# One softmax loop over sixteen heads in a two-block transformer kernel, with its transpositions spread over the steps around it

## The reference

```python
def attn_mixer(h, w_in, ...):
    c_q, c_kv, k_r, q_b, k_b, v_b = jnp.split(h @ w_in, IN_SPLITS, axis=-1)
    q = rms_norm_2(c_q, g_cq) @ w_uq                 # 8 heads x 96, rope on 32
    kv = rms_norm_2(c_kv, g_ckv) @ w_ukv             # 8 heads x (64 + 64)
    ...
    q = rms_norm_2(q, g_qn_mla) * (MLA_QK ** -0.5)
    k = rms_norm_2(k, g_kn_mla)
    o_mla = causal_attention_blocks(q, k, v)
    qm = rms_norm_2(heads(q_b), g_qn_moba) * (MOBA_HEAD_DIM ** -0.5)
    km = rms_norm_2(heads(k_b), g_kn_moba)
    o_moba = moba_attention(qm, km, heads(v_b))      # with 256 tokens one block:
    return concat(o_mla, o_moba) @ w_o               # plain causal softmax attention
```

## Time and profile before

| what | value |
|---|---|
| median of 3 runs | 920.19 us (920.02 to 922.31) |
| the profiled execution's own time | 920.32 us |
| its span | 918.5 us, 12101 instructions |
| PE busy | 872.7 us (95%) |
| DVE, ACT, POOL busy | 573.6, 441.0, 106.9 us |
| mean granted clock of PE | 0.993 of full speed |

### The profile page before, as it was taken

One profiled execution on the slowest core, in us unless ns is written; L12 is line 12 of the kernel. 1 busy time (PEld: TensorE's weight loads), 2 busy tenths in 40 slices (PEclk: granted clock), 3 DMA queues, 4 the chain that ended last, 5 costly groups with the idle time before them and its releaser, 6 DMA issues.

```text
span 918.5 us, 12101 instructions
## 1 busy us (share of the span) xinstructions
PE 872.7 (95%) x5003; PEld 720.8 (78%) x5003; DVE 573.6 (62%) x707; ACT 441.0 (48%) x584; POOL 106.9 (12%) x73
## 2 busy tenths in 40 slices
PE   6999999898999999899999999999689999999997
PEld 5888788787887877778778777887678878888886
DVE  4685475775343768855777777776776565555552
ACT  5634466566853645534544445442154554444441
POOL 1000000211000013105033333331000000000000
PEclk9999999999999999999999999999799999999999
DMA  8826466353022627306446555656775555555521
GB/s 298 294 97 229 161 210 223 139 187 135 1 58 101 249 92 254 113 1 205 157 147 213 199 173 189 207 202 170 203 273 187 183 180 187 184 183 183 183 92 46
DMA packets 67248, 155.87 MB, mean 170 GB/s; under 512 B 3017, under 2 KB 6826, under 8 KB 66938
## 3 DMA queue, kind: packets, MB, share of 16 engines
q1 hardware_dynamic: 63888, 146.28, 46.7%
q0 software_dynamic: 2224, 7.67, 2.5%
q10 hardware_dynamic: 1082, 1.16, 0.6%
HBM read 146.70 MB, written 7.34 MB: 168 GB/s over the span
## 4 chain that ended last, share of the span: by engine, by line
PE 74%; DVE 15%; ACT 5%; issue 3%; DMA 2%; POOL 1%; ACTq 0%; DVEq 0%
PE bank L643 20%; PE bank L645 20%; PE bank L644 20%; DVE wlo L1454 4%; ACT whi L1112 2%; PE bank L636 2%; PE bank L744 1%; DMA ring<-in_w_in 1%; PE bank L904 1%; DVE wlo L1449 1%; DVE hT_lo L1437 1%; PE bank L955 1%; PE bank L787 1%; PE bank L717 1%; DVE work L1629 1%
## 5 line engine op out<-in xcount | busy, mean ns | idle before, releaser
L1454 DVE TENSOR_TENSOR wlo<-ring,whi 128x2048 fp32r<-128x2048 f32 (+1 forms) x105 | 255.2, 2434 | 162.3 <-ACT whi L1112 162.1
L1112 ACT ACTIVATE whi<-ring 128x2048 fp32r<-128x2048 f32 (+1 forms) x105 | 200.4, 1908 | 228.8 <-PE bank L645 187.0
L643 PE MATMUL bank<-whi,hT_hi 128*128 128x512 f32 (+1 forms) x736 | 291.2, 396 | 4.8 <-DVE hT_lo L2018 2.3
L645 PE MATMUL bank<-whi,hT_lo 128*128 128x512 f32 (+1 forms) x736 | 287.0, 390 | 0.0
L644 PE MATMUL bank<-wlo,hT_hi 128*128 128x512 f32 (+1 forms) x736 | 286.9, 390 | 0.0
L643 PEld LDWEIGHTS bank<-whi,hT_hi 128*128 128x128 f32 x736 | 139.0, 189 | 34.1 <-issue 3.5
L645 PEld LDWEIGHTS bank<-whi,hT_lo 128*128 128x128 f32 x736 | 138.7, 188 | 28.8
L644 PEld LDWEIGHTS bank<-wlo,hT_hi 128*128 128x128 f32 x736 | 139.1, 189 | 27.2 <-issue 0.2
L643 PE MATMUL bank<-whi,hidT_hi 128*128 128x512 f32 x256 | 100.6, 393 | 1.1 <-DVE hidT_lo L1955 1.1
L645 PE MATMUL bank<-whi,hidT_lo 128*128 128x512 f32 x256 | 99.7, 390 | 0.0
L644 PE MATMUL bank<-wlo,hidT_hi 128*128 128x512 f32 x256 | 99.7, 389 | 0.0
(11 more groups left out here) (273 smaller groups left out, 952.8 us busy)
## 6 DMA issues: line engine op xcount, KB each, us to landing
ring<-in_w_ff SPq DMA_DIRECT2D x64, 1024.0 KB, 5.3
ring<-in_ple_gate_w SPq DMA_DIRECT2D x8, 1024.0 KB, 5.2
ring<-in_w_kv SPq DMA_DIRECT2D x8, 1024.0 KB, 7.0
ring<-in_b_w_in SPq DMA_DIRECT2D x8, 1024.0 KB, 5.0
ring<-in_a_w_in SPq DMA_DIRECT2D x7, 1024.0 KB, 13.0
ring<-in_w_in SPq DMA_DIRECT2D x6, 1024.0 KB, 5.5
ring<-in_w_glu SPq DMA_DIRECT2D x6, 1024.0 KB, 6.3
ring<-in_a_w_out SPq DMA_DIRECT2D x4, 1024.0 KB, 5.8
```

Of the source, the lines that this page charges most:

```text
L643: pe.matmul(bank_cols, high[:, at[0], at[1]], w_high, start=first, stop=False)
L645: return pe.matmul(bank_cols, low[:, at[0], at[1]], w_high, start=False, stop=last)
L1112: act.activation(whi[at], raw_rows(g), ACT.Copy).then_inc(high_made, 1)
L1454: dve.tensor_tensor(wlo[at], raw_rows(g), whi[at], ALU.subtract).then_inc(low_made, 1)
```

## The change

- `AHEAD` is 3: the probabilities of head n are turned in step n + 3 (before, n + 2), and the values follow in step n + 4.
- One loop of 20 steps covers 16 heads, the MLA heads first. The MoBA heads' scores are made two at a time in the even steps 8 to 14, their products alternating between the upper and lower 64 rows.
- The MLA queries and keys are turned in pairs of heads: tiles 0 and 1 inside the product "wv", between the two token tiles of its second half (`amid`), tiles 2 and 3 at steps 1 and 2. ACT empties all query tiles, DVE all key tiles. The MoBA tiles are turned at steps 4 to 7, one a step, all in bank 7 and all emptied by ACT.
- ACT loads the table of the exponential ahead of `refill("wv", 0)` (`preload_act_table_set`).
- On DVE the squares of the MLA keys go ahead of `refill("wq", 1)`, the scaling of the MLA queries ahead of `refill("wk", 0)`, that of the MLA keys ahead of `refill("wk", 1)`; the means of the MoBA keys go ahead of the loop, and `refill("wv", 0)` moves from ahead of the loops to the end of step 10.
- The banks of "wv" are 2 and 3 (before, 1 and 2). The turn of the bank list has advanced less, so the output's turned tiles come to banks 1 to 4.

```diff
+AHEAD = 3
+MOBA_TURNS = {4: ("qmoba", 0), 5: ("qmoba", 1), 6: ("kmoba", 0), 7: ("kmoba", 1)}
...
+def soft_plan(u):
+
+    u.add(("wv", 0, 0), "a", bank=2)
+    for k in range(2):
+        u.add(("T", "qmla", k), "a", bank=4 + 2 * k)
+        u.add(("T", "kmla", k), "v", bank=5 + 2 * k)
+    u.add(("wv", 0, 1), "a", bank=3)
+    for i in range(2 * MH + AHEAD + 1):
+        if i < MH:
+            u.add(("scores", i), "a", bank=i % 4)
+        elif i < 2 * MH and i % 2 == 0:
+            u.add(("scores", i), "a", bank=i % 4)
+            u.add(("scores", i + 1), "a", bank=i % 4 + 1)
+        if i in (1, 2):
+            u.add(("T", "qmla", 1 + i), "a", bank=2 + 2 * i)
+            u.add(("T", "kmla", 1 + i), "v", bank=3 + 2 * i)
+        if AHEAD <= i < 2 * MH + AHEAD:
+            u.add(("probsT", i - AHEAD), "v", bank=4 + (i - AHEAD) % 2)
+        if i > AHEAD and (i - AHEAD - 1) % 4 == 3:
+            m = (i - AHEAD - 1) // 4
+            u.add(("soft_out", m), "v", bank=6 + m % 2)
+        if i in MOBA_TURNS:
+            name, k = MOBA_TURNS[i]
+            u.add(("T", name, k), "a", bank=7)
...
+                            if amid and t == 0:
+                                amid()
...
+            def early_turns():
+                soft_turns(0)
+                soft_turns(1)
+
+            product("wv", 0, "wv", amid=early_turns)
...
+            def moba_scores(i):
+
+                pair = [begin(("scores", i + odd)) for odd in range(2)]
+                rows = [slice(HD * odd, HD * odd + HD) for odd in range(2)]
+                c = (i - MH) // 2
+                tq, tk = turned_qk["moba"]
+                emptied(("T", "qmoba", c // 2))
+                emptied(("T", "kmoba", c // 2))
+                for b, r in zip(pair, rows):
+                    pe.matmul(b[:, 0:P], tq[r, c, 0:P], tk[r, c, 0:P], start=True, stop=False, skip_group_check=True)
+                for b, r in zip(pair, rows):
+                    pe.matmul(b[:, P:P + S], tq[r, c, P:S], tk[r, c, :], start=False, stop=False, skip_group_check=True)
+                for odd, b in enumerate(pair):
+                    score_masks(i + odd, b)
...
+            for i in range(2 * MH + AHEAD + 1):
+                if i < MH:
+                    mla_scores(i)
+                elif i < 2 * MH and i % 2 == 0:
+                    moba_scores(i)
+                if i in (1, 2):
+                    soft_turns(1 + i)
+                if i >= AHEAD and i - AHEAD < 2 * MH:
+                    probs_turned(i - AHEAD)
+                if i > AHEAD:
+                    soft_values(i - AHEAD - 1)
+                if i in MOBA_TURNS:
+                    name, k = MOBA_TURNS[i]
+                    turn(name, qb if name == "qmoba" else kb, units=(k,),
+                         ready=lambda k: pe.wait_ge(heads_normed, 4 if name == "qmoba" else 7))
+            turn("o2", h, ready=lambda k: emptied(("soft_out", k)))
...
+            refill("wk", 0)
+            tokens_out("wk", 0, kb, 2)
+            refill("wk", 1)
+            act.preload_act_table_set("natural_log_exp_and_others")
+            refill("wv", 0)
+            copy_out(("wv", 0, 0), vb[:, 0, :], None, rstd[:, 2, 0:1])
+            turned_out("qmla", [(turned_qk["mla"][0], "qn_mla", True)], units=(0, 1), width=MQK)
+            copy_out(("wv", 0, 1), vb[:, 1, :], None, rstd[:, 2, 1:2])
+            for i in range(2 * MH):
...
+            row_squares("kmla")
             refill("wq", 1)
-            row_means("kmla")
+            row_sums("kmla")
+            row_scale("qmla", 3 + 2)
             refill("wk", 0)
-            row_scale("qmla", 3 + 2)
+            row_scale("kmla", 3 + 3)
             refill("wk", 1)
-            row_scale("kmla", 3 + 3)
-            refill("wv", 0)
-
-            for n, kind in enumerate(("mla", "moba")):
-                moba = kind == "moba"
-                tq, tk = turned_qk[kind]
-                if moba:
-                    turned_out("qmoba", [(tq, "qn_moba", True)], units=(0,))
-                    turned_out("kmoba", [(tk, "kn_moba", True)], units=(0,))
-                else:
-                    turned_out("qmla", [(tq, "qn_mla", True)], width=MQK)
-                    turned_out("kmla", [(tk, "kn_mla", True)], width=MQK)
-                for i in range(MH + 3):
-                    if i < MH:
-                        b = filled(("scores", kind, i))
-                        dve.tensor_reduce(nmax[:, n, i, 0:1], b[:, 0:P], AX_X, ALU.max, negate=True)
-                        dve.tensor_reduce(nmax[:, n, i, 1:2], b[:, P:384], AX_X, ALU.max, negate=True)\
-                            .then_inc(max_ready, 1)
-                    if 2 <= i < MH + 2:
-                        b = filled(("probsT", kind, i - 2))
-                        dve.tensor_copy(probsT[:, (i - 2) % 3, :], b[:, 0:384]).then_inc(dve_emptied, 1)
-                    if kind == "mla" and i == 2:
-                        emptied(("wk", 0, 1))
-                        row_means("kmoba")
-                    if kind == "mla" and i == 5:
-                        row_scale("kmoba", 7)
-                    if i >= 3 and (i - 3) % 4 == 3:
-                        k = (i - 3) // 4
-                        b = filled(("soft_out", kind, k))
-                        emptied(("scores", kind, 4 * k + 3))
-                        link(dve.reciprocal(rden[:, n, 4 * k:4 * k + 4, :], den[:, n, 4 * k:4 * k + 4, :]))
-                        at = (512 if moba else 0) + 256 * k
-                        dve.tensor_tensor(h[:, :, at:at + 256].rearrange("p t (n d) -> p n t d", d=HD),
-                                          b[:, :].rearrange("p (n t d) -> p n t d", n=4, t=NT),
-                                          rden[:, n, 4 * k:4 * k + 4, :].unsqueeze(3).broadcast_to([P, 4, NT, HD]),
-                                          ALU.mult).then_inc(dve_emptied, 1)
+            turned_out("kmla", [(turned_qk["mla"][1], "kn_mla", True)], units=(0, 1), width=MQK)
+            emptied(("wk", 0, 1))
+            row_means("kmoba")
...
+            for i in range(2 * MH + AHEAD + 1):
+                if i < 2 * MH:
+                    maxima(i)
+                if i in (1, 2):
+                    turned_out("kmla", [(turned_qk["mla"][1], "kn_mla", True)], units=(1 + i,), width=MQK)
+                if i >= AHEAD and i - AHEAD < 2 * MH:
+                    b = filled(("probsT", i - AHEAD))
+                    dve.tensor_copy(probsT[:, (i - AHEAD) % 3, :], b[:, 0:384]).then_inc(dve_emptied, 1)
+                if i == 3:
+                    row_scale("kmoba", 7)
+                if i > AHEAD and (i - AHEAD - 1) % 4 == 3:
+                    soft_out((i - AHEAD - 1) // 4)
+                if i == MH + 2:
+                    refill("wv", 0)
             turned_low("o2", None)
             refill("wv", 1)
```

More of the change, by code:

```diff
@@ L210, in plan @@
     gemm(u, "wk", 1, "a")
[L211 to L214, removed]
[L215 to L221 removed]
+    soft_plan(u)
     turned_in_two(u, "o2")
@@ L650, in part_views, with product @@
                 return (v[at].rearrange("p (k n) -> p k n", n=width) for v in (whi, wlo))
-            def product(stage, nb, name, width=512, turned_by=None, gelus=False, between=None, first=None, pieces=False):
+            def product(stage, nb, name, width=512, turned_by=None, gelus=False, between=None, first=None, pieces=False,
+                        amid=None):
                 banks = [begin((stage, nb, t)) for t in range(NT)]
@@ new lines, in mla_scores @@
+            def mla_scores(i):
+                b = begin(("scores", i))
+                tq, tk = turned_qk["mla"]
+                emptied(("T", "qmla", i // 2))
+                emptied(("T", "kmla", i // 2))
+                pe.matmul(b[:, 0:P], tq[0:MQK, i, 0:P], tk[0:MQK, i, 0:P], start=True, stop=False, skip_group_check=True)
+                pe.matmul(b[:, P:P + S], tq[0:MQK, i, P:S], tk[0:MQK, i, :], start=False, stop=False,
+                          skip_group_check=True)
+                score_masks(i, b)
@@ new lines, in probs_turned, with soft_values @@
+            def probs_turned(n):
+                b = begin(("probsT", n))
+                emptied(("scores", n))
+                for k in range(3):
+                    last = pe.transpose(b[:, k * P:(k + 1) * P], probs[:, n % 3, k * P:(k + 1) * P], ident)
+                last.then_inc(pe_done, 1)
+            def soft_values(n):
+                name = ("soft_out", n // 4)
+                b = begin(name) if n % 4 == 0 else bank(name)
+                o = b[:, (n % 4) * P:(n % 4) * P + P]
+                emptied(("probsT", n))
+                a = probsT[:, n % 3, :]
+                vh = (vm if n < MH else vb)[:, :, n % MH * HD:(n % MH + 1) * HD]
+                pe.matmul(o[:, 0:HD], a[:, 0:P], vh[:, 0, :], start=True, stop=True)
+                pe.matmul(o[:, HD:P], a[:, P:S], vh[:, 0, :], start=True, stop=False)
```

(3 more changed lines are left out.)

122 lines of the change are left out of this document (45 added, 77 removed).

## The result

The changed kernel takes 914.66 us in the median of 12 runs (913.74 to 919.32), beside 923.01 for 12 runs of the kernel before (920.02 to 944.29); the ratio is 0.9907, with a 95% interval of 0.9883 to 0.9932. It is faster by about 0.9%. The forecast was 911.1 us, within 908.8 to 915.0. The profiled execution took 914.48 us. Ratios and intervals leave out executions that took over 1.5% longer than the fastest of their kernel (944.29 us here).

What follows compares the result with a forecast made beforehand. TensorE, busy for 95% of 918.5 us, was taken as the bound. Work of 32.2 and waits of 0.3, 1.9 and 0.5 from 370.3, then 2.2, start the projection at 407.4, not 416.6: 9.2 less, 911.1 us, range 908.8 to 915.0.

Steps and rivals of the forecast that it cites:

- PE's work, 32.2 us: TensorE's own work from the end of "wv" (370.33) to the last values, with MoBA scores in pairs: 32.2 us.
- The waits of steps 13 to 19: PE waiting late in the loop, where turned probabilities, copies and values follow closely: 0.5 us, bounds 0.2 and 1.5.
- The start: MLA transposes inside "wv" need no wait, their evictions lie under the product, and the holes of 374.0 to 384.0 close.
- The table load: The 1.28 us load at 376.11 moves to 362, where ACT has 3.00 us free.
- The pairs: Two heads' MoBA scores with alternating rows take 1.19 us, bounds 1.09 and 2.12; four pairs 4.8 against 8.5.
- Rival B: Pairs of MoBA scores bring nothing: 3.7 us more PE work, 913.9 us in all; chance 0.07.
- The fill at step 10: DVE's fill of "w_o" in the loop makes PE wait for copies 8 and 9: 1.9 us, bounds 0 and 3.0.
- Rival C: The fill in the loop finds room, as PE is late for another reason or DVE is quicker: 909.2 us; chance 0.1.
- The output's transposes: In banks 1 to 4, from the last values to the projection: 2.2 us, against 4.6 before.
- D: Weights of "w_o" or the FFN hold what follows, so the end doesn't move: 918 to 920 us; chance 0.04.
- E: The loop runs by handoffs, 2.37 us a step: 925 us; slower than before from 2.1 a step; chance 0.04.
- rival A: The clock falls at the loop's end or in the wait of steps 12 and 13: 912.8 us, twice 914.5; chance 0.2.

Runs made afterwards that it cites:

- second profile: The kernel before run again with nothing edited: 926.51 us, ratio 1.001; 74.02 us between the marks.
- third profile: The changed kernel run a third time with nothing edited: 915.75 us, ratio 0.9914 to the kernel before; 61.11 us between the marks.
- bank 7: The changed kernel with the four turned output tiles in banks 7, 0, 1, 2 in place of 1 to 4: 915.88 us, ratio 0.9909.
- new banks: The kernel before with only the turned output tiles' banks changed, from 7, 0, 1, 2 to 1, 2, 3, 4: 922.81 us, ratio 0.9991.

## Why the prediction was right, and where it was off

- **PE's work, 32.2 us, and the last values at 405.2.** Measured 407.00 for the start of the output's transposes; less 1.8 by which this execution is later at the first mark, 405.2. The total is right, two terms aren't. In the version with the fill at step 5, the stretch from the place of 370.33 (22.2 us behind the first mark) to the output's transposes is 33.1 us with one wait of 0.3, so PE's own work is 32.8. The waits of steps 13 to 19 (0.5 in the sum) aren't there: no hole over 0.15 us stands behind step 13 in this profile. The two misses cancel, which is luck.
- **The start.** No wait inside "wv", the holes of 374.0 to 384.0 gone. Right, and the bound was near: the first maximum followed at 374.86 right behind the key means. The cover named is what the transposes behind "wv" lack, at 1.68 us.
- **The table load.** Its move was right, the slack beside it wrong. The sum laid the first exponential, ready at 374.7, against step 3 at 377.3: 2.6 us, which would hide a load of 1.28. What step 3 waits for last is ACT's eviction of query tile 2, behind two heads' exponentials. It had 0.74 us of room in the changed kernel, and without the early load PE waits 0.4.
- **The pairs.** 1.10 us plus the gap, as the stick attention's row had it (1.09), on both sides of the doubt "two small tiles or one large". Rival B falls: without pairs 2.64 more.
- **The MoBA tiles' bank.** 0.28 for 0.3.
- **The fill at step 10.** 0.89 + 0.55 of visible holes; 1.82 by moving it to step 5. I had 1.9 (the first wait should read 4.4 - 3.4 = 1.0, not 1.1). Rival C falls, and what it named (room for the fill) exists at another step.
- **The output's transposes.** 2.2 us had been the sum from the last values to the projection; 407.00 to 409.18 is 2.18. The bank choice with its clock is worth 2.24 on the kernel before and 1.99 on the changed one.
- **Rivals D and E.** The stretch behind the second mark that holds "w_o" and the first FFN is as long as before (226.12 us, 226.16 before), so no weights hold it. The 20 steps from the first scores (373.89) to the output's transposes (407.00) take 1.66 us each, under the 2.1 of E; even with AHEAD = 2 the stage is only 0.56 longer.
- **The sum, 9.2 us between the marks.** 9.14 measured. Of this 1.16 is a fall that the first profile of the kernel before had and its second had not; without it 8.0.
- **The time, 911.1.** 914.66: here the prediction was off by 3.5 us, 0.3 inside the end of its range. The room at that end had been made for rivals A and B and for handoffs, and none of these came in the profile; that it held the time is luck. The step that failed is "from the projection to the end the kernel should be as long as before", together with the silence on what lies ahead of the changed stage: rival A looked for a fall of the clock "at the loop's end or in the wait of steps 12 and 13" alone. From the projection to the end the kernel is 1.6 us longer, which was to be the sign of D, but it lies in the state-space stage and goes with a longer piece of low clock; ahead of the first mark it is 1.8 us longer, by a fall in the stick attention. The fall in the stick attention is a matter of the execution: 8 of the 14 profiles have one there, the kernel before's second among them, and its first had been a lucky one. The piece in the state-space stage isn't shown to be (below).
- **The ratio** came out as forecast, 911.1 / 920.32 = 0.990 and 0.9907 measured, because the median of the kernel before also rose, from 920.19 in 3 runs to 923.01 in 12, which the forecast had no reason for. The lowest times of all runs of the two programs, 920.02 and 910.78, are 9.2 apart.
- **What I took for the kernel before** was one profile with a fall of 1.16 us in the stage. Its second profile had one of about 6.5. Part of what the change brings in the medians may be that its loop gives the clock fewer holes to fall at: of the eleven profiles of the changed kernel and its variants eight show no fall between the marks, and the three that do (third profile, bank 7, no early table load) show one of 1.6 us or less. With three profiles of the family before (two falls) that isn't shown, and the granted clock of whole executions doesn't settle it: the medians are 0.983 for the kernel before and 0.988 for the changed one in one set of rounds, 0.991 and 0.987 in another.

Open is the long piece in the state-space stage. In all three profiles of the changed kernel the clock is 0.50 there for 20 to 24 us without a break (640.6 to 661.1, 635.8 to 659.7, 638.5 to 662.4); in none of the other eleven, which have two or three pieces of 3 to 10 us each. From the second mark to the end the changed kernel takes 503.2, 503.5 and 503.2 us, the kernel before 501.7 and 502.0 and 502.6 with new banks. Whether the piece belongs to this kernel's timing or came thrice by chance was not settled: some of the 1.6 us may be the change's own. Shorter pieces aren't always cheaper, though: the version with the fill at step 5 had 505.2 us behind the projection in one profile and 501.8 in the other, and AHEAD = 2 had 506.1; so the execution matters too.

## What to carry to other kernels

Lay the in-order queues side by side from the rows and look for the step where one engine's long instruction meets another's short steps; a fill moved by five steps was worth 1.8 us, and one index of a bank list 2.0 to 2.2, half of it a fall of the clock that doesn't come in every execution. Ask who ended each wait: the slack of the table load was reckoned against the wrong instruction. Ask of every PSUM bank that opens a new phase who emptied it last, since a hole of one us there can also cost the clock behind it. Where the clock falls in different places from one execution to the next, compare stages between marks and not whole times, and profile the kernel before more than once.

## What the runs showed of the hardware that was not expected

**A busy PE doesn't always bring the clock back.** In the second profile of the kernel before PE was busy for all of 388.0 to 395.0 and the clock stayed at 0.50 (the windows above), and in the changed kernel it did for 20 us:

```profile
640.80:661.00 20.20, 19.60 (x290) 18.87 (x292) 16.58 (x31) 0.00 (x0) 0.00 (x0) 0.50 0.73 214
661.00:665.00 4.00, 4.00 (x72) 3.99 (x69) 3.86 (x8) 0.67 (x1) 0.00 (x0) 0.99 1.03 397
```

19.60 of 20.20 us busy with 290 matmuls at the level of 1.2 GHz, and 2.4 GHz behind it. The Trainium skill (TensorE: Matmul & The Clock Gate, What's actually happening) says that the throttled state is the default and activity releases it; of these two stretches of small matmuls that isn't true by busy time, and the measurement decides. A hole isn't enough for a fall either: the same hole of 1.02 us ahead of the output had a fall behind it in the first profile of the kernel before and none in the second, and the same two holes of steps 12 and 13 had one in the third profile of the changed kernel and none in the other two.

**A fill is twice as long beside POOL's elementwise work.** The same 128x2048 fill on DVE took 2.28 us in the loop, and 5.92 and 4.74 in the projection with the fill behind the output, where POOL's elementwise work ran. The changed kernel has such a row, too:

```profile
411.54 10.00 DVE L1508 TENSOR_TENSOR wlo<-ring,whi 128x2048 fp32r<-128x2048 f32 x2 [0.53 <-ACT whi L1165]
```

Of the 103 fills of this length in the changed kernel, the 89 with POOL idle take 2.28 or 2.29 us each, with the DMA engines full or idle and with ACT busy or idle; nine beside POOL's long elementwise instructions take 4.2 to 5.3. Not all of POOL's work does this: beside its power of 128x16 at 363.66 a fill took 2.31. This accounts for the 2.04 us of the late fill: had its first fill taken 2.3 us in place of 5.92, it would have been done 3.6 us sooner. The Trainium skill (GPSIMD Engine Reference, Specifications) says that POOL shares its SBUF interfaces with DVE and contends with DVE instructions that have two SBUF inputs, as this one has; the rows agree for the long elementwise instructions, and give the price: 1.9 to 3.6 us on 2.3. That the shared interface is the cause was not tested apart.
